# Two gathers per expert group: the V rows of a group are asked for behind the U rows of the next group

## What is computed

```python
def peer(x, wq, subkeys, U, V):
    def block(xt):
        q = (xt @ wq).reshape(blk, PK_HEADS, 2, PK_DQ // 2)
        ...
        top_s, sel = lax.top_k(cand_s, PK_TOPK)
        idx = jnp.take_along_axis(cand_i, sel, axis=-1)
        gate = jax.nn.softmax(top_s, axis=-1)
        act = jax.nn.gelu(jnp.einsum('thed,td->the', U[idx], xt), approximate=False)
        return jnp.einsum('the,thed->td', (gate * act), V[idx])
```

## Time and profile before

| | |
|---|---|
| median of 3 runs | 2187.84 us (2187.05 to 2196.26) |
| the profiled execution | 2200.15 us, span 2198.0 us |
| granted clock of TensorE, mean | 0.908 |
| first gather from U to last gather from V | 767.5 to 2178.3 us of the span |
| busy in the span: PE, DVE, POOL, ACT | 83%, 67%, 62%, 21% |

### The profile page before, as it was taken

The page is one execution under the profiler, slowest core; times in us unless marked ns, Lnnn a source line. Parts: engine busy times, 40 slices in busy tenths (PEclk is TensorE's granted clock), DMA queues, the critical chain, the costliest instruction groups (busy, mean ns, idle before and its releaser), DMA issues.

```text
span 2198.0 us, 21368 instructions
## 1 busy us (share of the span) xinstructions
PE 1819.0 (83%) x7178; PEld 990.1 (45%) x7178; DVE 1469.2 (67%) x3313; ACT 463.3 (21%) x1116; POOL 1354.3 (62%) x1289
## 2 busy tenths in 40 slices
PE   8968568898885768899877789977989977899876
PEld 5833237687662523344433334533444533336332
DVE  2667634546556377777777787687777587785666
ACT  0121120000001113332223233222332222121220
POOL 2795712222220077777777777777777777776775
PEclk9989777999897779999999999999999998997988
DMA  7453121121113199999999999999999999999997
GB/s 259 131 180 105 58 72 35 49 73 44 54 40 137 68 364 409 409 404 365 394 374 409 394 408 377 404 386 400 365 383 404 371 391 389 408 389 341 368 395 295
DMA packets 179244, 620.99 MB, mean 283 GB/s; under 512 B 20436, under 2 KB 23892, under 8 KB 178752
## 3 DMA queue, kind: packets, MB, share of 16 engines
q0 software_dynamic: 160672, 581.00, 69.4%
q1 hardware_dynamic: 18464, 38.63, 4.8%
HBM read 613.89 MB, written 5.59 MB: 282 GB/s over the span
## 4 chain that ended last, share of the span: by engine, by line
PE 22%; POOL 16%; DMA 12%; DVE 11%; issue 6%; ACT 2%; DVEq 0%; POOLq 0%
PE ps L1538 16%; DMA p_Ur<-in_peer_u_dram,p_idx 11%; POOL p_Ur L1335 8%; POOL p_Vr L1335 7%; DVE p_Ur L1795 6%; PE ps L1464 2%; PE ps L1492 2%; ACT p_dg L1658 1%; ACT p_gel L1652 1%; PE ps L1429 1%; DVE p_x L1678 0%; DVE p_junk L1682 0%; DVE p_x L1693 0%; DMA w_out<-in_w_out_dram 0%; DVE p_wgt L1804 0%
## 5 line engine op out<-in xcount | busy, mean ns | idle before, releaser
L1538 PE MATMUL ps<-p_Vr,p_dg 128*128 128x512 f32 x2048 | 991.4, 641 | 209.3 <-ACT p_dg L1658 198.1
L1795 DVE CUSTOM_DVE_ANT_0 p_Ur<-p_Ur,p_x 128x1024 f32<-128x1024 f32 x512 | 617.4, 1225 | 267.9 <-DMA p_Ur<-in_peer_u_dram,p_idx 257.4
L1538 PEld LDWEIGHTS ps<-p_Vr,p_dg 128*128 128x128 f32 x2048 | 411.0, 206 | 754.1 <-issue 494.4
L1335 POOL DMA_INDIRECT p_Ur<-in_peer_u_dram,p_idx x512 | 521.7, 1019 | 270.9 <-issue 155.8
L1335 POOL DMA_INDIRECT p_Vr<-in_peer_v_dram,p_idx x512 | 544.6, 1064 | 168.3 <-issue 120.8
L1652 ACT ACTIVATE p_gel<-p_dot 128x4 f32<-128x4 f32 x128 | 26.3, 205 | 936.6 <-DVE p_dot L1795 936.6
L1658 ACT ACTIVATE p_dg<-table_long,p_wgt 128x128 f32<-128x128 f32 x512 | 163.5, 390 | 29.4 <-DVE p_wgt L1804 29.4
L940 POOL DMA_INDIRECT vring<-in_cache_v_dram,idx x64 | 61.5, 961 | 150.0 <-PE ps L836 148.3
L300 PE MATMUL ps<-w_ring,xT 128*128 128x512 f32 (+1 forms) x224 | 105.6, 628 | 6.5 <-ACT kv L402 6.5
L275 PE MATMUL ps<-xT,w_ring 128*128 128x268 f32 x448 | 104.6, 398 | 6.3 <-DMA xT<-in_xT_dram 6.3
L424 POOL DMA_INDIRECT kv<-in_cache_k_dram,idx x56 | 60.8, 1086 | 74.1 <-PE ps L284 35.2
(11 more groups left out here) (359 smaller groups left out, 2110.6 us busy)
## 6 DMA issues: line engine op xcount, KB each, us to landing
w_ring<-in_w_in_dram SPq DMA_DIRECT2D x5, 2048.0 KB, 9.0
p_Ur<-in_peer_u_dram,p_idx POOLq DMA_INDIRECT x512, 6.6
p_Vr<-in_peer_v_dram,p_idx POOLq DMA_INDIRECT x512, 6.8
w_out<-in_w_out_dram SPq DMA_DIRECT2D x2, 2048.0 KB, 10.6
wq<-in_pk_wq_dram SPq DMA_DIRECT2D x2, 2048.0 KB, 20.4
xT<-in_xT_dram SPq DMA_DIRECT2D x4, 536.0 KB, 6.2
kv<-in_w_in_dram SPq DMA_DIRECT2D x1, 2048.0 KB, 17.5
w_out<-q_rows POOLq DMA_DIRECT2D x8, 256.0 KB, 3.7
```

Source lines behind the costliest of these rows:

```text
L1335: pool.indirect_dma_start(out=dst, out_offset=None, in_=io[table], in_offset=bass.IndirectOffsetOnAxis(ap=at, axis=0)).then_inc(s_to, 16)
L1538: mm = pe.matmul(acc[:, a, :], dg[:, j % DG, :], Vr[:, j % RV, a * 512:(a + 1) * 512], start=(at == 0), stop=(at == SLOTS - 1), skip_group ...
L1795: ins = dve.tensor_tensor_reduce(Ur[:, r, :], Ur[:, r, :], x, 1.0, 0.0, ALU.mult, ALU.add, dot[:, r:r + 1])
```

## The change

`group` is split in two. `rows_u` issues the four U rows of a group and `rows_v` the four V rows, each with the waits that it had. In the loop over the groups POOL now issues the U rows of group g and behind them the V rows of group g - 1. After the loop come the V rows of the last prompt group, then the U rows of both sample groups, then their V rows. The buffers, the semaphores, the values waited for, the number of gathers and the programs of the other engines stay as they are.

```diff
-            def group(g, index):
+            def rows_u(g, index):
                 for j in range(G * g, G * g + G):
                     if j == G * g and j >= R:
                         pool.wait_ge(s_dot, g - R // G + 1)
                     row("peer_u", Ur[:, j % R, :], index(j), s_u[j % R])
+
+            def rows_v(g, index):
                 for j in range(G * g, G * g + G):
                     if j >= RV:
                         pool.wait_ge(s_free, j - RV + 1)
                     row("peer_v", Vr[:, j % RV, :], index(j), s_vv[j % RV])
...
                     for grp in range(GPP):
-                        group((PARTS * t + part) * GPP + grp, lambda j: idx[:, t % 2, j - SLOTS * t:j - SLOTS * t + 1])
+                        g = (PARTS * t + part) * GPP + grp
+                        rows_u(g, at_prompt)
+                        if g:
+                            rows_v(g - 1, at_prompt)
+            end = PARTS * NT * GPP
+            rows_v(end - 1, at_prompt)
             pool.wait_ge(s_rs, 16)
             for half in range(2):
-                group(PARTS * NT * GPP + half, lambda j: idr[:, j - SLOTS * NT:j - SLOTS * NT + 1])
+                rows_u(end + half, at_sample)
+            for half in range(2):
+                rows_v(end + half, at_sample)
```

More of the change, by code:

```diff
@@ L1346, in group, with at_prompt, at_sample @@
                     row("peer_v", Vr[:, j % RV, :], index(j), s_vv[j % RV])
+            def at_prompt(j):
+                t = j // SLOTS
+                return idx[:, t % 2, j - SLOTS * t:j - SLOTS * t + 1]
+            def at_sample(j):
+                return idr[:, j - SLOTS * NT:j - SLOTS * NT + 1]
             for t in range(NT):
```

## The result

The changed kernel takes **2261.66 us** (median of 4 executions, 2260.15 to 2264.97), the kernel before 2187.45 (4 executions, 2181.61 to 2196.26): a ratio of 1.0338, with an interval of 1.0301 to 1.0375. The forecast was 2223, with a range up to 2248. The direction holds, the size doesn't, and the time lies outside the range.

The account below looks back on a forecast made before the run. POOL's gathers were taken to set the pace, slowed when DVE comes late and runs its dots back to back. Terms 33.6 + 5 - 6 + 2 gave +35 us on the median 2187.84, so 2223 us, range 2186 to 2248.

Parts of the forecast that it names:

- U rows, and the DMA queues: U row gathers on POOL: blocks of four stay one group's period apart and land as before; nothing gained, nothing lost.
- V rows one period later, PE behind them, DVE behind PE: Tile 0: V rows asked for 10.23 us later, PE's scores later, DVE's maxima 9.34 us later, next dots 8.2 us late.
- How long that lasts: DVE's delay makes g = 5 to 18 packed in tiles 0 to 2: 42 groups, about 13 already so, 29 new.
- packed: A group whose four dots on DVE run back to back, starts within 3.6 us; forecast to slow POOL's gathers beside it.
- Price of one: Each new packed group lengthens the 10.24 us period by 1.16 us; 29 give +33.6 us, bounds 23.5 and 42.9.
- The wait for the dots: POOL's U rows waiting for late dots on DVE: +5 us, bounds 0 and 30.
- Waits for V buffers: POOL's waits for free V buffers, 12.1 us before: -6 us, bounds -12 and 0.
- Ends: Start and end of the program, with PE's last product and the last layer norm about 1 us later: +2 us, bounds 0 and 4.
- The sum: All terms together: 33.6 + 5 - 6 + 2 = +35 us, put on the median 2187.84; bounds +14 to about +60.
- Much slower, about 2257: Rival: POOL's wait for dots becomes the bound, if DVE's delays pass about 10 us in tiles 0 and 1; +69, chance 0.09.
- Faster: Rival: V rows no longer hold up U rows, if DVE's wait for PE stays below 1.9 us a group; 2173, chance 0.09.
- No change: Rival: DVE comes late but its dots don't hold POOL's gathers; only small terms, +1, 2189 us, chance 0.19.

Follow-up runs that it names:

- e4: Kernel before, with two useless one-input reductions added on DVE behind the dots of g = 4 to 17 in tiles 0 to 2: 2229.51 us, ratio 1.0197.
- e1: Kernel after, with DVE waiting for each dot of a group to be written before starting the next: 2199.75 us, ratio 1.0053 to the kernel before.
- e2: Kernel before, with DVE waiting for each dot of a group to be written before starting the next: 2168.60 us, ratio 0.9904.
- e8: Kernel before, with a tiny one-input reduction (2 columns, 0.15 us) on DVE between the dots of a group: 2163.47 us, ratio 0.9905.
- e3: Kernel after, with POOL waiting only for the dot of the row whose buffer it needs, not the whole group: 2259.93 us, ratio 1.033 to before.
- e5: Kernel after, with DVE waiting for each dot before the next and POOL waiting for dots row by row: 2169.07 us, ratio 0.9919 to before.
- e7: Kernel after, without the attention of prompt tiles 1 to 3 on PE, ACT and DVE: 2207.29 us, ratio 1.008 to the kernel before.
- e6: Kernel before, without the attention of prompt tiles 1 to 3 on PE, ACT and DVE: 2171.27 us, ratio 0.9906.
- e10: Kernel before with a tiny reduction between the dots, the same kernel as e8 run again with 10 executions: 2164.78 us, ratio 0.9911.

## Why the prediction was right in direction and short in size

*U rows, and the DMA queues.* Right: in tile 3, from g = 4 to 11, the dots of two groups start 10.22 to 10.24 us apart, at 409 GB/s as before.

*V rows one period later, PE behind them, DVE behind PE.* Right in kind and near in size. The maxima wait in all 24 cases, and the first of each pair starts 8.1 us after the last dot has ended, 4.7 to 12.7, where I had some 9. I had the dots of g = 14 in tile 0 start 8.2 us late, at 930.78; they start at 935.76, 13.2 us after the 922.59 of before. Of these, 6.1 us are that the first row itself lands later (928.60 instead of 922.45), as the gathers had already lost time; the dots start 7.2 us behind this landing. At g = 11 of tile 0 it is 12.2 us.

*How long that lasts: the first step that failed.* The 42 groups g = 5 to 18 of tiles 0 to 2 are packed, all of them, as forecast, and between the dots of g = 5 and those of g = 19 the surplus of these tiles rose by 33.3 us, against 33.6 in my sum. This near agreement is partly luck: 36 and not 29 are new (of "about 13" that I took as packed or slow already, 6 were packed and 6 more had 0.9 to 1.5 us of surplus), and one costs less than I took. What failed is that the sum has no term for the rest of the program. The surplus rose by 14.6 us there, with 13 more packed groups: 6 in the other groups of tiles 0 to 2 (g = 24 and 28 above all), 6 in tile 3 (g = 16, 20 to 22, 29, 30) and one with the sample tokens. That makes 36 + 13 = 49 new groups, not 29.

*Price of one.* A little too high: 47.9 us of new surplus for 49 groups is 0.98 us, in e4 0.96, against my 1.16. 49 x 0.98 = +48 instead of 29 x 1.16 = +33.6. That dots hold the gathers at all, the premise of this term and against the rule cited with it, is shown by e1, e2 and e8. But "packed" is only where it shows most: each dot holds what starts within it, and in 71 of the 78 packed groups one or two gathers are caught near the start of a dot and take over 1.5 us.

*The wait for the dots: the second step that failed.* Taken at +5, measured 21.1 us. I had worked out 21 us for the steps of the attention "without any relief" and some 10 more at the layer norm, 31 in all, and took nearly all of it off again, since packed groups stretch the slack. The relief was real but partial. The rows that follow the dots of the attention's steps (U rows of g = 7, 13 and 16, as at 910.31) waited 10.4 us above their 0.30, half of the figure; those that follow a layer norm (g = 23 in tiles 0 to 2, g = 15 in tile 3, at 2020.65) waited 10.7, all of it. That the total is 21 like the first figure is chance. e3 shows that it can't be had back alone, and e5 that it is worth 31 us once the dots are spaced.

*A wait that I hadn't priced:* DVE's own for the gelu, `DVE p_wgt`, went from 38.4 to 72.8 us, the longest from 4.0 to 11.8; the three longest, 28.7 us together, are in tile 3 at 2087.99, 2103.95 and 2193.62. The gelu waits there behind other work of ACT: in the stretch of the gathers its copies of the queries (L1647) wait 81.1 us for PE's products, where they waited 12.7. So a late PE reaches DVE a second time, through ACT and `prep`. It isn't the attention, since e7 without it has 69.0 us of this wait, and e6 36.8. No run took this wait out by itself.

*Waits for V buffers.* -6 forecast, -7.6 measured. *Ends.* +2 forecast, +3.5 measured; the last products come late as said, for the earlier trace rows:

```profile
2236.70 16.80 PE L1569 MATMUL ps<-p_Vr,p_wsel 128*8 128x512 f32 x32 [4.69 <-DMA p_Vr<-in_peer_v_dram,p_idr]
```

*The sum.* 48 + 21 - 8 + 3.5 = 65 us between the profiled executions, 74 between the medians, against the +35 forecast. The two failed steps, 14.6 us outside the 42 groups and 16.1 of wait, are that difference of 30. My range missed it by a step of its own: the upper bounds of the terms, 42.9 + 30 + 0 + 4, make +77, and I stopped at about +60 with no more reason than that they don't all come at once (the lower ones make +11.5, not +14). I put the difference on the median and noted that the profiled execution lay 12 us above it. That is where another 10 us went: the profiled execution of before, 2200.15 us, is one of the longest of that kernel (2176.63 to 2203.18 over the study), that of after is the longest of four that lie close together (2260.15 to 2264.97), so the difference of two traces was smaller than that of the medians.

*The rivals.* "Much slower, about 2257" was nearest. Its condition, delays on DVE past 10 us in tile 0 and 1 too, was met (the dots of g = 11 start 12.2 and 11.4 us after their first row has landed), and its size too, 69 against the 65 of the traces. It isn't quite its mechanism: POOL's wait for the dots is no new bound by itself (e3), the packed groups carry most of it. "Faster" failed at its own condition. "No change" failed with e1. What I held for it, that something beside DVE holds POOL a little in quiet groups, was wrong too: 25.8 of the 26.3 us of surplus beside the dots of the 70 quiet groups of before lie in gathers that start within a dot.

## What to carry to other kernels

Where one engine issues gathers and another takes long passes over SBUF tiles, look at where within a pass each gather starts, not only at how busy the engine is: when the two periods fit together, gather after gather can be caught at its worst point. A tiny instruction between the passes, or a wait, shifted that and gave 1% here. When a change makes an engine late, count what that costs over the whole program, and not only in the stretch where it begins; and take off from a new wait no more relief than a row shows. Costs that meet on one engine don't add: taken out alone, the wait by row gave 2 us in the median, with the other cost gone 31.

## What the runs showed of the hardware

- An indirect gather of 128 rows of 4 KB takes GpSimd 0.93 to 0.94 us undisturbed. If it starts 0.05 to 1.05 us after the start of one of VectorE's dots (1.22 us, two SBUF inputs, 128x1024), it ends 2.02 to 2.05 us after that start: 1723 of 1723 in 13 traces. So it takes up to 2.00 us, with one dot as with four in a row.
- Back-to-back dots (starts 1.14 to 1.15 us apart) catch one gather after another at that point. Starts 1.27 us apart (e1) or a 0.15 us instruction with one small input between the dots (e8, e10; starts 1.22 us apart) bring most gathers back to 0.94 to 0.98 us; with the filling VectorE is never idle between them.
- A one-input reduction of the same length (e4, 1.22 us) held none of the 84 gathers that started 0.75 to 0.86 us into it. No gather started earlier in one.
- The Trainium skill (SBUF — State Buffer, Who interferes with whom) says that a two-input VectorE instruction contends with a GpSimd instruction that reads SBUF, and infers that descriptor generation isn't stalled by it. These gathers are stalled (1.98 and 1.99 us in the kernel after, the same two 0.93 in e1). An indirect gather reads its indices from SBUF, so the first half of the rule may cover it where the inference doesn't; no run here tells which interface it is.
- Between 53 and 70 us of surplus stay in every kernel with spaced or filled dots. Of these, 42 to 55 us lie in gathers that start 0.05 to 1.05 us into a dot, most of them in the first of a group. Open: what the gather waits for within the pass, and what makes the executions of one kernel differ by up to 27 us.
